# Layer norms of a hybrid decoder trunk: root spread by transposes, group products reordered, x kept in float32 for three FFNs, last centring shared

## What is computed

```python
def layer_norm(x, g, b):
    mu = jnp.mean(xf, -1, keepdims=True)
    var = jnp.mean(jnp.square(xf - mu), -1, keepdims=True)
    return ((xf - mu) * lax.rsqrt(var + LN_EPS) * g + b).astype(x.dtype)
...
x = LN(alpha*x + 0.5*SwiGLU_a(x))
x = LN(alpha*x + Mixer(x))          # layer 0: sliding-window attention (SWA), layer 1: NSA
x = LN(alpha*x + CrossAttn(x, mem)) # 4 heads into 256 memory tokens
x = LN(alpha*x + 0.5*SwiGLU_b(x))
```

## Time and profile before

| | |
|---|---|
| median of 3 runs | 2382.92 us (2380.39 to 2385.24) |
| the profiled execution | 2381.28 us, span 2379.0 us |
| mean granted TensorE clock | 0.985 |
| weights and inputs moved | 204.92 MB, mean 86 GB/s |

### The profile page before, as it was taken

How to read it: one execution, slowest core, us unless ns; L and a number is a source line. 1 busy time by engine, 2 the same in 40 slices (tenths; PEclk the granted TensorE clock), 3 DMA queues, 4 the chain that set the end, 5 groups by cost and what they waited for, 6 DMA issues and landing times.

```text
span 2379.0 us, 28084 instructions
## 1 busy us (share of the span) xinstructions
PE 2273.8 (96%) x10964; PEld 1863.5 (78%) x10964; DVE 764.3 (32%) x1561; ACT 821.2 (35%) x1398; POOL 1154.9 (49%) x694
## 2 busy tenths in 40 slices
PE   8999999889899999999999999989989899999997
PEld 6888888667788888888788888776657787888886
DVE  3111125454526111104311113645554436111115
ACT  3322233543434322223322223445553433222222
POOL 5454445567546644444544444334446645644441
PEclk9999999999999999999999999999999999999998
DMA  5332323112413333333333332210003312333331
GB/s 179 98 96 91 103 85 114 54 36 86 128 54 106 98 98 95 100 94 98 93 98 98 92 103 89 82 43 19 19 19 98 107 45 79 108 96 94 102 92 59
DMA packets 57731, 204.92 MB, mean 86 GB/s; under 512 B 6912, under 2 KB 7040, under 8 KB 57088
## 3 DMA queue, kind: packets, MB, share of 16 engines
q1 hardware_dynamic: 55728, 196.63, 27.5%
q10 hardware_dynamic: 1872, 6.50, 0.8%
HBM read 201.01 MB, written 2.10 MB: 85 GB/s over the span
## 4 chain that ended last, share of the span: by engine, by line
PE 89%; POOL 3%; DVE 3%; ACT 2%; issue 2%; DMA 0%; SPq 0%; ACTq 0%; DVEq 0%
PE bank L1208 25%; PE bank L1210 25%; PE bank L1209 25%; POOL w_lo L401 3%; PE bank L1428 2%; PE bank L1464 2%; PE bank L1401 1%; PE bank L1253 1%; PE bank L1254 1%; PE bank L1255 1%; DVE t L933 1%; PE bank L1402 1%; ACT w_hi L539 1%; DVE f L1129 1%; PE bank L1441 0%
## 5 line engine op out<-in xcount | busy, mean ns | idle before, releaser
L401 POOL TENSOR_TENSOR w_lo<-w_raw,w_hi 128x1024 fp32r<-128x1024 f32 (+1 forms) x379 | 902.4, 2385 | 954.9 <-ACT w_hi L539 954.9
L1208 PE MATMUL bank<-x_hi,w_hi 128*128 128x512 f32 x1688 | 665.4, 394 | 20.7 <-POOL w_lo L401 12.1
L1209 PE MATMUL bank<-x_lo,w_hi 128*128 128x512 f32 x1688 | 662.1, 392 | 0.0
L1210 PE MATMUL bank<-x_hi,w_lo 128*128 128x512 f32 x1688 | 662.0, 392 | 0.0
L539 ACT ACTIVATE w_hi<-w_raw 128x1024 fp32r<-128x1024 f32 (+1 forms) x379 | 390.9, 1035 | 525.7 <-PE bank L1210 509.2
L1208 PEld LDWEIGHTS bank<-x_hi,w_hi 128*128 128x128 f32 x1688 | 319.9, 190 | 88.1 <-POOL w_lo L401 11.5
L1208 PE MATMUL bank<-h_hi,w_hi 128*128 128x512 f32 x960 | 379.2, 395 | 2.3 <-DVE h_lo L1150 1.4
L1210 PE MATMUL bank<-h_hi,w_lo 128*128 128x512 f32 x960 | 374.1, 390 | 0.0
L1209 PE MATMUL bank<-h_lo,w_hi 128*128 128x512 f32 x960 | 374.1, 390 | 0.0
L1210 PEld LDWEIGHTS bank<-x_hi,w_lo 128*128 128x128 f32 x1688 | 319.5, 189 | 67.6
L1209 PEld LDWEIGHTS bank<-x_lo,w_hi 128*128 128x128 f32 x1688 | 320.0, 190 | 62.7
(11 more groups left out here) (204 smaller groups left out, 2400.5 us busy)
## 6 DMA issues: line engine op xcount, KB each, us to landing
w_raw<-w_dram SPq DMA_DIRECT2D x315, 512.0 KB, 3.6
w_raw<-w_dram SPq DMA_DIRECT2D x64, 448.0 KB, 3.3
f<-mem_dram ACTq DMA_DIRECT2D x3, 1024.0 KB, 5.0
t<-x_dram ACTq DMA_DIRECT2D x4, 512.0 KB, 8.4
out_dram<-t SPq DMA_DIRECT2D x8, 256.0 KB, 2.0
f<-cmp_w_dram ACTq DMA_DIRECT2D x1, 1024.0 KB, 7.4
cw<-cmp_w_dram ACTq DMA_DIRECT2D x1, 96.0 KB, 3.4
lng<-ln_g_dram ACTq DMA_DIRECT2D x1, 32.0 KB, 3.2
```

What stands on the lines that cost most here:

```text
L401: pool.tensor_tensor(w_lo[:, slot(s), 0:n * P], w_raw[:, s % RAW, 0:n * P], w_hi[:, slot(s), 0:n * P].bitcast(F32), ALU.subtract).then_inc ...
L1208: pe.matmul(dst, w_hi[:, slot(s), w], m_hi[:, k, :], start=k == 0, stop=False)
L1209: pe.matmul(dst, w_hi[:, slot(s), w], m_lo[:, k, :], start=False, stop=False)
L1210: last = pe.matmul(dst, w_lo[:, slot(s), w], m_hi[:, k, :], start=False, stop=k == n - 1)
```

## The change

- `mean4` and its copy and product on DVE go; ACT squares the means straight from the bank (`msq_ready`). The constants lose their scaling by D.
- The four diagonals and L1320 go; PE transposes `rstd4[:, i:i+1]`, read 128 times over as a repeated column. These transposes stand behind chunks 0 and 1 of fill 1 instead of behind all of it (for a token-major fill: behind its first half).
- `together` issues, per chunk, the three w_hi products with x_hi once `xhi_ready` allows, then the three w_lo products of two chunks before, then those with x_lo once `x_ready` allows. w_hi of A, B, C is waited for at chunk 0, w_lo at chunk 2.
- In norms 2, 3 and 6 (`KEEPS`) ACT also writes the full float32 x to `t`, POOL makes `x_lo` as t minus x_hi, and the FFN that follows doesn't call `base`.
- DVE centres one chunk ahead instead of two. In norm 7, ACT copies the spread mean to SBUF after the first centring, and POOL centres chunks 4 to 7 (`LAST`).

```diff
@@ POOL, ffn
-                        if part == 0 and st.ln and n >= 2 and n < 6:
+                        if part == 0 and st.ln - 1 not in KEEPS and st.ln and n >= 2 and n < 6:
@@ POOL, new norm
+            def norm(st):
+                first = (st.fill[-1][2] if st.fill else st.out[-1])[-1] + 1
+                for j in range(KC):
+                    feed(first + min(j + 1, 3))
+                    pool.wait_ge(x_full, kept(stages[st.ln + 1], j))
+                    pool.tensor_tensor(x_lo[:, j, :], t[:, j, :], x_hi[:, j, :].bitcast(F32),
+                                       ALU.subtract).then_inc(x_ready, 1)
...
+                if st.keeps:
+                    norm(st)
+                if st is final:
+                    pool.wait_ge(mean_here, 1)
+                    for j in LAST:
+                        pool.wait_ge(dev, KC * st.ln + j + 1)
+                        pool.tensor_tensor(t[:, j, :], t[:, j, :], mean_sb, ALU.subtract).then_inc(cent_pool, 1)
@@ ACT, norm
-                act.wait_ge(stat, 8 * st.ln + 3)
-                act.activation(std4, var4, ACT.Sqrt, scale=1.0 / D ** 2, bias=eps[:, 0:1]).then_inc(std_ready, 1)
+                act.wait_ge(mean_tok, st.ln + 1)
+                act.activation(msq4, bank[B_SHIFT][:, 0:4], ACT.Square).then_inc(msq_ready, 1)
+                act.wait_ge(stat, 2 * st.ln + 1)
+                act.activation(std4, var4, ACT.Sqrt, bias=eps[:, 0:1]).then_inc(std_ready, 1)
+                if st is final:
+                    act.wait_ge(cent, n0 + 1)
+                    act.activation(mean_sb, bank[B_MEAN][:], ACT.Copy).then_inc(mean_here, 1)
...
+                    if st.keeps:
+                        act.activation(t[:, j, :], t[:, j, :], ACT.Identity, bias=b).then_inc(x_full, 1)
@@ DVE, norm
-                dve.wait_ge(mean_tok, st.ln + 1)
-                dve.tensor_copy(mean4, bank[B_SHIFT][:, 0:4]).then_inc(stat, 1)
-                dve.wait_ge(stat, c0 + 1)
-                dve.tensor_tensor(msq4, mean4, mean4, ALU.mult).then_inc(stat, 1)
...
-                dve.wait_ge(stat, c0 + 4)
-                for i in range(NT):
-                    dve.tensor_scalar(diag[:, P * i:P * i + P], ident[:], rstd4[:, i:i + 1], None,
-                                      ALU.mult).then_inc(stat, 1)
...
                 centre(0)
-                centre(1)
                 fill(1)
                 dve.wait_ge(rstd_rep, st.ln + 1)
                 for j in range(KC):
                     scale(j)
-                    if j and st is not final:
+                    if j and st is not final and not st.keeps:
                         lo(j - 1)
-                    if j + 2 < KC:
-                        centre(j + 2)
+                    if j == 0 and st is final:
+                        dve.wait_ge(mean_here, 1)
+                    if j + 1 < KC and not (st is final and j + 1 in LAST):
+                        centre(j + 1)
@@ PE, together
-                for k in range(KC):
-                    pe.wait_ge(x_ready, KC * st.ln + k + 1)
+                behind = 2
+                for k in range(KC + behind):
+                    w = slice(k * P, (k + 1) * P)
+                    if k < KC:
+                        pe.wait_ge(xhi_ready, KC * st.ln + k + 1)
+                        for s, dst in group:
+                            if k == 0:
+                                pe.wait_ge(hi_ready, s + 1)
+                            pe.matmul(dst, w_hi[:, slot(s), w], x_hi[:, k, :], start=k == 0, stop=False)
                     for s, dst in group:
-                        chunk(s, dst, x_hi, x_lo, k, KC)
+                        m = k - behind
+                        if m == 0:
+                            pe.wait_ge(lo_ready, s + 1)
+                        if m >= 0:
+                            last = pe.matmul(dst, w_lo[:, slot(s), m * P:(m + 1) * P], x_hi[:, m, :], start=False,
+                                             stop=m == KC - 1)
+                            if m == KC - 1:
+                                last.then_inc(slab_done, 1)
+                    if k < KC:
+                        pe.wait_ge(x_ready, KC * st.ln + k + 1)
+                        for s, dst in group:
+                            pe.matmul(dst, w_hi[:, slot(s), w], x_lo[:, k, :], start=False, stop=False)
@@ PE, norm
                 if len(st.fill) > 1:
-                    fill_slabs(st, 1)
+                    fill_slabs(st, 1, range(0, 2))
+                pe.wait_ge(stat, 2 * st.ln + 2)
                 for i in range(NT):
-                    pe.wait_ge(stat, 8 * st.ln + 5 + i)
-                    last = pe.matmul(bank[B_RSTD][:, P * i:P * i + P], ones[:], diag[:, P * i:P * i + P], start=True,
-                                     stop=True)
+                    last = pe.transpose(bank[B_RSTD][:, P * i:P * i + P], rstd4[:, i:i + 1].to_broadcast([P, P]), ident[:])
                 last.then_inc(rstd_rep, 1)
+                if len(st.fill) > 1:
+                    fill_slabs(st, 1, range(2, KC))
```

More of the change, by code:

```diff
@@ L69, in __init__ @@
         self.slab, self.fill0, self.sem = {}, 0, {}
+        self.keeps = ln in KEEPS
 class Unit:
@@ L292, in build @@
         m8, s8, r8, q8 = (small[:, 96 + 8 * i:104 + 8 * i] for i in range(4))
[L293 removed]
+        msq4, var4, std4, rstd4 = (small[:, 128 + 4 * i:132 + 4 * i] for i in range(4))
         cst = small[:, 148:150]
@@ L361, in slot, with kept, based @@
             return s % SLOTS
+        def kept(st, j):
+            return KC * KEEPS.index(st.ln - 1) + j + 1
+        def based(st, j):
+            return KC * len([n for n in range(1, st.ln) if n - 1 not in KEEPS]) + j + 1
         def out_reads(st, part, j):
@@ L860, in out_chunk @@
                 tj = t[:, j, :]
-                if part == 0 and st.ln:
-                    dve.wait_ge(base_in, KC * (st.ln - 1) + j + 1)
+                if part == 0 and st.ln - 1 in KEEPS:
+                    dve.wait_ge(x_full, kept(st, j))
+                elif part == 0 and st.ln:
+                    dve.wait_ge(base_in, based(st, j))
                 if not last:
@@ L931, in scale @@
                 def scale(j):
-                    dve.wait_ge(cent, n0 + j + 1)
+                    if st is final and j in LAST:
+                        dve.wait_ge(cent_pool, LAST.index(j) + 1)
+                    else:
+                        dve.wait_ge(cent, n0 + j + 1)
                     dve.scalar_tensor_tensor(out=t[:, j, :], in0=t[:, j, :], scalar=lng[:, st.ln, j:j + 1],
@@ L968, in norm @@
                     scale(j)
-                    if j and st is not final:
+                    if j and st is not final and not st.keeps:
                         lo(j - 1)
-                    if j + 2 < KC:
-                        centre(j + 2)
+                    if j == 0 and st is final:
+                        dve.wait_ge(mean_here, 1)
+                    if j + 1 < KC and not (st is final and j + 1 in LAST):
+                        centre(j + 1)
                     if j in (2, 4, 6):
                         fill(j // 2 + 1)
-                if st is not final:
+                if st is not final and not st.keeps:
                     lo(KC - 1)
@@ L1276, in out_slab, with fill_slabs @@
                     chunk(s, bank[OUT_BANK[j % 3]][:], h_hi, h_lo, k, n)
-            def fill_slabs(st, m):
+            def fill_slabs(st, m, chunks=range(KC)):
                 lay, c, ss = st.fill[m]
@@ L1291, in fill_slabs @@
                     for n, s in enumerate(ss):
-                        for k in range(KC):
+                        for k in chunks:
                             chunk(s, b[:, MEM * n:MEM * (n + 1)], mem_hi, mem_lo, k, KC)
@@ L1297, in fill_slabs @@
                 for i in range(2):
-                    last = token_major(ss, b[:, 256 * i:256 * i + 256], i, mem_hi, mem_lo, 256)
-                last.then_inc(slab_done, 2)
+                    if 4 * i in chunks:
+                        last = token_major(ss, b[:, 256 * i:256 * i + 256], i, mem_hi, mem_lo, 256)
+                if KC - 1 in chunks:
+                    last.then_inc(slab_done, 2)
             def norm(st):
```

19 lines of the change are left out of this document (12 added, 7 removed).

## The result

The changed kernel takes 2369.57 us (median of 4 runs, 2368.96 to 2370.82), the kernel before 2383.88 beside it (2380.39 to 2385.24): a ratio of 0.9946 with an interval of 0.9933 to 0.9958. That is 12.9 us less by the ratio, against 14.9 forecast; the time forecast was 2368, with a range of 2361 to 2377. The profiled execution took 2370.82 us with a span of 2368.9; the spans differ by 10.1 us.

A forecast was written before the change was run, and what follows sets the result against it. PE's matmuls, busy 2273.8 of 2379.0 us, were taken as the bound; norm terms -1.6 - 7.5 + 0 - 2.8 = -11.9 and clock -3 gave -14.9, by the median 2368 us; range 2361 to 2377.

The forecast's parts named there:

- The earlier root: Norm 3: transposes behind a quarter of fill 1 let the first scaling start at about 1130.0 instead of 1132.22.
- Rival (a): Norms 0, 1 and 5: POOL and landings set the ring, an earlier root moves nothing; -2, 2381 us; chance 0.08.
- Rival (d): Groups of three slabs: third hi as late as third lo was, new order gives nothing; -10, 2373 us; chance 0.16.
- Rival (c): Norms 2, 3 and 6, chunks 1 to 7: x_lo on POOL sets the pace; +15, 2398 us; chance 0.04.
- Rival (b): Norm windows: the clock gives back its whole bound; -21, 2362 us; chance 0.12.
- Statistics: All norms: four transposes (0.60 us) replace eight passes (1.06), 0.45 less PE work; removing L917 gives 0.3 at most.
- Norms 2, 3 and 6: Kept x: POOL's order of x_lo and w_lo sets the cost; net +0.8, +0.2 and -1.0 us.
- norm 2's +0.8: Norm 2: fourth slab's hi comes late, x_lo(2) ready at about 768.1, PE waits 3 us; net +0.8 us.
- Norms 0, 1 and 5: Earlier root and new order shorten w_lo waits, later slab release costs 0.9 us; net -2.7, -1.9 and -2.9.
- Norms 4 and 6: Norm 4: PE starts 3 us earlier, waits about 1.8 at chunk 1, net -1.6; norm 6: net -1.0.
- Norm 7: Last window: scaling 0 at about 2365.9 instead of 2366.91, fewer centrings between scalings (1.8 less); net -2.8 us.
- Clock: Norm windows: of 15.6 us lost to the lower clock, -3 us taken, bounds -9 to +2.

The follow-up runs named there:

- the repeated run: The changed kernel run once more, word for word, with nothing changed against it: 2369.39 us, ratio 0.9951 to the kernel before.

## Why the prediction was right, and which terms were not

**Direction and mechanism held.** The earlier root carries most of the gain. With the rest of the change in place but the root late, the total is that of before (0.9999); with the root and its new statistics alone, two thirds of the gain are there. The parts don't simply add up: with the late root five norms stay shorter than before, and norms 2 and 3, the attention stages and the later release take it back. The first scaling came 4.0 us after the first statistics product in norm 3; forecast was 2.2 us earlier, measured 2.6. Rival (a), that POOL and the landings hold norms 0, 1 and 5, falls: the windows of norms 0 and 5 are 6.7 and 4.6 us shorter, and the w_lo waits shrank. Rival (d) falls too: the new order is worth some 4 us (12.9 less 8.8), the amount that would have been missing, though in norm 1 the third slab's w_hi is late (a wait of 2.3 us) nearly as w_lo was (2.7). Rival (c) falls: PE's waits on POOL's x_lo end with chunk 2. Rival (b) is half true, see the clock below.

**Statistics.** Four transposes took 0.60 us in norm 3, as forecast from the earlier trace rows. An estimate by the Trainium skill (TensorE: Matmul & The Clock Gate, Part 4: PE-mode transpose), four at 275 ns one behind the other, was 1.10; the trace does not agree with that sum for four in a row.

**Norms 2, 3 and 6.** POOL's order cost what was said: in norm 3 waits of 0.73 and 1.93 us were forecast as 0.9 and 2.2, and of the third, 1.5, nothing shows, since the products ahead of it ran at the lower clock (three of w_lo 1.48 us, from 1138.76 in the order of time) and lasted until x_lo was there; the clock's loss hid in that wait. In norm 2 the wait was 2.69 for a forecast 3. **The mis-sized term is norm 2's +0.8**: it measured +2.7, because the clock fell behind that wait (0.94 in the window; 0.89 and +4.0 in the repeated run) where it was 1.00 before. I had put the clock's part of norm 2 into a bound only. That the 24 additions are worth nothing in the FFNs is confirmed in both directions.

**Norms 0, 1 and 5.** To the next work they gave 5.8, 1.7 and 3.7 us; forecast 2.7, 1.9 and 2.9 without the clock. Norm 0 had 3.6 us of missing clock and norm 5 1.9, now both none: less these, 2.2, 1.7 and 1.8. The late end of the three slabs cost its 0.9 each (3.3 before the value product, 2.5 twice before the queries). **A term was missing**: behind the 2.5 us waits the cross-attentions ran 1.5 us longer with a clock of 0.98 instead of 1.00. That the late end brings it is shown by all the profiles taken together. The six with the late end (the changed kernel twice, nothing kept, root late, fourth slab's w_lo last, centrings on DVE) have 104.1 to 104.2 us in the first cross-attention five times of six and 102.9 in the second five times of six. The six with the old order or the early end have 102.6 to 102.8 and 101.4 to 101.6 each time. It is not certain in each execution: the repeated run has the first at 102.6, the run with the late root the second at 101.4. In the text on record one clause is wrong: the windows of the earlier trace rows for norms 0, 1 and 5 end with the group and do not take in the wait behind it.

**Norms 4 and 6.** 3.7 and 2.9 us instead of 1.6 and 1.0. Their windows went from a clock of 0.88 to 1.00 and from 0.82 to 0.93, which by the prediction's own count (3.5 us, and 5.0 less 1.7) is nearly all of it: without the clock norm 4 gave 0.2 us and norm 6 nothing. Of norm 4's wait of 2.8, 1.4 is left (forecast 1.8). Its group of 72 takes 1524.3 - 1505.25 = 19.1 us; less that 1.4 it is 17.6, where 72 products of 0.227 would be 16.3. The rest are gaps between the first chunks too short for the list of waits. I had not counted them.

**Norm 7**: 2.0 instead of 2.8. In the order of time, the first row from the kernel before, the others from the changed one:

```profile
2364.85 2.01 PE L1320 MATMUL bank<-diag,ones 128*128 128x128 f32 x8 [0.15 <-DVE diag L925]
...
2355.53 1.71 PE L1371 MATMUL bank<-f,ones 128*128 128x512 f32 x2
2357.03 1.06 PE L1376 MATMUL bank<-ident,small 128*128 128x128 f32 x4
2358.12 0.75 DVE L969 SCALAR_TENSOR_TENSOR t<-t,lng,bank 128x512 f32<-128x512 f32 x1 [0.17 <-PE bank L1376]
2358.66 4.96 POOL L558 TENSOR_TENSOR t<-t,f 128x512 f32<-128x512 f32 x4 [21.07 <-ACT f L670]
2359.50 0.75 DVE L969 SCALAR_TENSOR_TENSOR t<-t,lng,bank 128x512 f32<-128x512 f32 x1
...
2362.26 3.38 DVE L969 SCALAR_TENSOR_TENSOR t<-t,lng,bank 128x512 f32<-128x512 f32 x5
```

The first scaling comes 4.4 us after the first statistics product, 5.1 before: 0.7 us earlier where I had 1.0. At the lower clock of this stretch the four transposes took 1.06 us where the eight passes had taken 2.01, but the product that spreads the mean now ran at the lower clock too, 1.71 us instead of 1.10. Scaling and centring take 1.38 a pair (2358.12 to 2359.50), not 1.26. The centring of the next chunk now stands directly ahead of the scaling that needs it; centred two ahead the pair took 1.25. First to last scaling is 6.8 us, forecast 6.4, before 8.2. POOL's four were hidden, as forecast.

**Clock.** Counted as in the prediction (stretch times what is missing), the seven windows had 15.6 us and have 5.1 (1.8 in norm 2, 1.6 in norm 3, 1.7 in norm 6): 10.5 back, more than rival (b)'s bound of 9, against the 3 I took. Without it the seven norms gave 4.5, forecast 9.1. Outside the windows 6.4 went the other way: 1.5 in each cross-attention, 2.5 in SWA, 0.9 in NSA. The sum of both, 4, is near the forecast's 3, though not for a reason I had. So the right total rests in part on two errors that cancel. Nor is the count exact: it sets a stretch's idle time at the lower clock down as lost too. The share of SWA and NSA is no effect of the change that these runs establish: the same program differs by 1.0 and 2.1 us there between two executions.

**Still open**: why the clock falls behind some waits of some 2.5 us and, in the same program, not behind others; what makes SWA vary (173.5 to 182.1 us among these kernels, the longest with a clock of 0.90) and PE's idle time in NSA; and where the gains of nothing kept and of the fourth slab's w_lo last lie beyond the 7.3 and 4.6 us of their norms. No experiment was made on these.

## What to carry to other kernels

In an in-order queue, count a reordering at both ends: what starts earlier in front, and which buffer is released later behind. The two small orders that the change got wrong (one conversion ahead of a product's operand on POOL, three slabs ending together) cost more together, 17 us (29.5 less 12.9), than the change gained. And where waits of 2 to 3 us are made or removed, price them with the lower clock that may follow, 1.5 to 2 us apiece in these traces, instead of leaving that to a bound.

## What the runs showed of the hardware

- A wait of 2.5 to 2.7 us can be followed by a stretch at the lower of the two clock levels: behind the wait of 2.69 in norm 2 (window clock 0.94 instead of 1.00), and behind the 2.5 before L1614, where the cross-attention grew from 102.6 to 104.1 us (0.98 instead of 1.00). The program run again had this in one cross-attention and not in the other.
- Four float32 transposes of 128x128 in a row took 0.60 us at the full clock (norm 3) and 1.06 at the lower one (norm 7).
- DVE's scaling, which reads a bank, took 0.75 us beside POOL's centring as it did without; POOL's four took 4.96. L917 with both inputs in SBUF took 0.89 us beside POOL's w_lo; in norms 5 and 7 of the same trace, with nothing on POOL, it took 0.16.
- On DVE a scaling that needs the result of the centring just ahead of it cost 0.12 us more than with another operation in between: 1.38 us a pair, with POOL busy beside it or idle, against 1.25 to 1.26.
